# Attention's end: the second output weight unit split in one piece, recurrent high parts in every second step, three rows of h reloaded later

## What is computed

```
q, k, v, xr, gr = jnp.split(hl @ w_in, splits, axis=-1)
att = neighbourhood_attention(heads(q), heads(k), heads(v), kc, vc, rpb)
...
rec, rec_c = bidir_rglru(xr, xc, ...)
y = jnp.concatenate([att, rec * jax.nn.gelu(gr)], axis=-1) @ w_out
...
h = h + g1 * y
h = h + g2 * swiglu(modulate(rmsnorm(h, norm2_g[l]), sh2, sc2), ffn_w_gu[l], ffn_w_down[l])
```

## Time and profile before

| | |
|---|---|
| median of 3 runs | 2519.69 us (2513.82 to 2519.84) |
| profiled execution: its time, its span | 2521.1 us, 2519.0 us |
| PE busy, share of the span | 2442.0 us, 97% |
| DVE, ACT, POOL busy | 1125.8, 525.9, 1058.0 us |
| granted TensorE clock, mean | 0.986 of full speed |

### The profile page before, as it was taken

One profiled execution on the slowest core, in us unless ns is written; L12 is line 12 of the kernel. 1 busy time (PEld: TensorE's weight loads), 2 busy tenths in 40 slices (PEclk: granted clock), 3 DMA queues, 4 the chain that ended last, 5 costly groups with the idle time before them and its releaser, 6 DMA issues.

```text
span 2519.0 us, 29518 instructions
## 1 busy us (share of the span) xinstructions
PE 2442.0 (97%) x11190; PEld 1997.2 (79%) x11190; DVE 1125.8 (45%) x1447; ACT 525.9 (21%) x805; POOL 1058.0 (42%) x507
## 2 busy tenths in 40 slices
PE   7999999989899999999999999999899999999999
PEld 3778878878788888888887788887688888888887
DVE  6566648855744444422223534246622222222224
ACT  2444438861200000000002200002200000000003
POOL 3233336888533344444333233432533333333340
PEclk8999999999999999999999899999899999999999
DMA  9433366523323333211111011111211111111111
GB/s 290 156 130 131 136 174 137 102 96 106 108 95 115 117 117 106 94 42 49 42 50 51 26 42 50 50 50 34 59 47 46 49 43 50 42 49 50 50 34 67
DMA packets 223197, 206.54 MB, mean 82 GB/s; under 512 B 40119, under 2 KB 193427, under 8 KB 222611
## 3 DMA queue, kind: packets, MB, share of 16 engines
q1 hardware_dynamic: 216643, 186.64, 25.2%
q10 hardware_dynamic: 5904, 16.78, 1.8%
q0 software_dynamic: 576, 2.10, 0.2%
HBM read 185.20 MB, written 20.28 MB: 82 GB/s over the span
## 4 chain that ended last, share of the span: by engine, by line
PE 90%; DVE 5%; issue 2%; ACT 1%; DMA 1%; POOL 0%; SPq 0%; DVEq 0%; POOLq 0%; ACTq 0%
PE bank L757 28%; PE bank L759 27%; PE bank L758 27%; PE bank L889 1%; DVE probs L1659 1%; PE bank L945 1%; PE bank L818 1%; DVE sumsq L1378 1%; PE bank L971 1%; PE bank L970 1%; PE bank L932 1%; PE bank L789 1%; ACT probs L1262 1%; PE bank L933 1%; DVE h L1421 1%
## 5 line engine op out<-in xcount | busy, mean ns | idle before, releaser
L591 POOL TENSOR_TENSOR w_hi<-raw,ones 128x1024 fp32r<-128x1024 f32 x184 | 361.6, 1965 | 1221.3 <-PE bank L759 1166.0
L757 PE MATMUL bank<-act_hi,w_hi 128*128 128x512 f32 x2160 | 846.0, 392 | 3.5 <-DVE act_lo L1539 2.9
L758 PE MATMUL bank<-act_hi,w_lo 128*128 128x512 f32 x2168 | 847.5, 391 | 0.0
L759 PE MATMUL bank<-act_lo,w_hi 128*128 128x512 f32 x2160 | 843.0, 390 | 0.0
L757 PEld LDWEIGHTS bank<-act_hi,w_hi 128*128 128x128 f32 x2160 | 407.4, 189 | 91.0 <-issue 2.8
L758 PEld LDWEIGHTS bank<-act_hi,w_lo 128*128 128x128 f32 x2168 | 409.4, 189 | 84.3
L759 PEld LDWEIGHTS bank<-act_lo,w_hi 128*128 128x128 f32 x2160 | 407.1, 188 | 85.4
L594 POOL TENSOR_TENSOR w_lo<-raw,w_hi 128x1024 fp32r<-128x1024 f32 x184 | 468.1, 2544 | 14.5
L1421 DVE SCALAR_TENSOR_TENSOR h<-bank,mods,h 128x512 f32<-128x512 f32 x432 | 319.5, 748 | 218.5 <-PE bank L759 217.3
L1699 DVE TENSOR_TENSOR hid_f<-silu_g,bank 128x512 f32<-128x512 f32 x88 | 60.5, 687 | 710.6 <-PE bank L759 709.4
L757 PE MATMUL bank<-hid_hi,w_hi 128*128 128x512 f32 x704 | 277.1, 394 | 3.6 <-DVE h L1421 3.4
(11 more groups left out here) (212 smaller groups left out, 2397.3 us busy)
## 6 DMA issues: line engine op xcount, KB each, us to landing
raw<-in_ffn_w_gu SPq DMA_DIRECT2D x88, 512.0 KB, 3.8
mod_in_f<-in_mod_w SPq DMA_DIRECT2D x48, 512.0 KB, 4.7
raw<-in_ffn_w_down SPq DMA_DIRECT2D x44, 512.0 KB, 3.6
mod_in_p<-in_mod_w SPq DMA_DIRECT2D x32, 512.0 KB, 6.7
raw<-in_o_w_in SPq DMA_DIRECT2D x24, 512.0 KB, 3.7
raw<-in_e_w_in SPq DMA_DIRECT2D x20, 512.0 KB, 4.9
mod_ring<-in_mod_w SPq DMA_DIRECT2D x16, 512.0 KB, 9.5
raw<-in_e_w_out SPq DMA_DIRECT2D x16, 512.0 KB, 3.7
```

What stands on the lines that cost most here:

```text
L591: nc.gpsimd.tensor_tensor(w_hi, raw[:, parity, :], ones[:, 0:1].to_broadcast([P, UNIT]), ALU.mult).then_inc(s_hi, 1)
L757: pe.matmul(dst, w_hi, x_hi, start=first, stop=False)
L758: pe.matmul(dst, w_lo, x_hi, start=False, stop=False)
L759: return pe.matmul(dst, w_hi, x_lo, start=False, stop=last)
```

## The change

Four things are moved. The second output unit gets a low part of its own, `o_lo1`, which lies on the key buffer of the even heads and on rows 4 and 5 of `h`; so POOL splits unit 1 in one piece, ahead of block 13, once the scores and minima of the seventh head are done. Unit 5 waits for block 14 instead of PE's second output group. ACT writes the recurrent high parts behind the exponentials of steps 51, 53, 55 and 57 instead of 55 to 58, and POOL takes each low part one place earlier relative to its blocks. SP reloads rows 3 to 5 of `h` only when PE has done its second output group, between the loads of units 3 and 4.

```diff
-        o_lo0 = at(91, "o_lo0", [P, UNIT], F32R)
+        o_lo = [at(91, "o_lo0", [P, UNIT], F32R), at(18.5, "o_lo1", [P, UNIT], F32R)]
...
-            return (o_hi[0][:], o_lo0[:]) if j == 0 else (o_hi[1][:], w_lo4[:, 1, :]) if j == 1 else w_slot(j % 4)
+            return (o_hi[j][:], o_lo[j][:]) if j < 2 else w_slot(j % 4)
...
             sp.wait_ge(s_sc, STEPS)
             sp.dma_start(h[:, 0:3, :], h_spill[:, 0:3, :]).then_inc(s_reload[0], 16)
-            sp.dma_start(h[:, 3:6, :], h_spill[:, 3:6, :]).then_inc(s_reload[1], 16)
             sp.wait_ge(s_pt, STEPS)
             sp.dma_start(h[:, 6:8, :], h_spill[:, 6:8, :]).then_inc(s_reload[2], 16)
             for j in range(2, 2 * FT):
                 load_unit(U_O + j, j % 2, column_unit(w_out, (j % FT) * P))
+                if j == 3:
+                    sp.wait_ge(s_out, 2)
+                    sp.dma_start(h[:, 3:6, :], h_spill[:, 3:6, :]).then_inc(s_reload[1], 16)
...
-                if j < 6:
-                    pool.wait_ge(*((s_pv, 3 * BLOCKS // 4), (s_min, STEPS - TT), (s_pv, BLOCKS - 1), (s_yf, BLOCKS),
-                                   (s_pv, BLOCKS - 1), used_o(1))[j])
+                if j == 0:
+                    pool.wait_ge(s_pv, 3 * BLOCKS // 4)
+                elif j == 1:
+                    pool.wait_ge(s_min, STEPS - TT)
+                    pool.wait_ge(s_sc, STEPS - TT)
+                elif j < 6:
+                    pool.wait_ge(*((s_yf, BLOCKS) if j == 3 else (s_pv, BLOCKS - 1)))
...
-                if STEPS - 10 <= j < STEPS - 6:
-                    lru_high(j - STEPS + 10)
+                if STEPS - 14 <= j < STEPS - 6 and j % 2 == 0:
+                    lru_high((j - STEPS + 14) // 2)
```

More of the change, by code:

```diff
@@ L692, in out_weight @@
                 pool.wait_ge(s_hi, U_O + j + 1)
[L693 to L699, removed]
                 nc.gpsimd.tensor_tensor(w_lo, raw[:, j % 2, :], w_hi, ALU.subtract).then_inc(s_split, 1)
@@ L716, in _ @@
                     split_values(head // 2)
+                if head == HEADS - 1:
+                    lru_low(0)
                 y_low(2 * head - 3)
             out_weight(0)
-            lru_low(0)
+            lru_low(1)
             y_scaled(BLOCKS - 4)
-            lru_low(1)
+            lru_low(2)
             y_low(BLOCKS - 4)
-            lru_low(2)
+            out_weight(1)
             y_scaled(BLOCKS - 3)
@@ L726, in _ @@
             y_low(BLOCKS - 3)
[L727 to L732, removed]
+            for g in (BLOCKS - 2, BLOCKS - 1):
+                y_scaled(g)
+                y_low(g)
             for j in range(2, 2 * FT):
```

## The result

The changed kernel takes 2530.80 us (median of 6 runs, 2528.99 to 2534.43) where the kernel before takes 2519.77 (6 runs beside it). The ratio is 1.0043, 95% interval 1.0033 to 1.0054: 8.3 to 13.6 us slower. 2528.9 had been forecast. The profiled execution, at 2528.99 us, is the fastest of the six; no trace was kept of the others.

What follows compares the result with a forecast made beforehand. PE (TensorE), with 90% of the span in the chain, was taken as the bound. Terms 10.8 - 2.8 + 0 + 1.2 = +9.2 us on the profiled 2521.1, 1.4 above the median, gave 2528.9 us; range 2523.5 to 2533.0.

Steps and rivals of the forecast that it cites:

- Step 1: At ACT's first recurrent high part, moved ahead of its wait for POOL's last key/query split: ACT stands 8.99 us, paid whole.
- Step 2: At ACT's cast of block 11's y: extra copy +1.03, recovery -1.5, clock +2.3; shift with stall +10.8, bounds +7.5 to +13.0.
- -1.5 recovered, +2.3 for the clock: Up to block 11: ACT's waits for DVE go in part, -1.5 us; PE's low clock behind the stall costs +2.3.
- Step 3: POOL's chain from block 11 to unit 0's second half on PE: 33.6 us where it was 36.4, so -2.8.
- Step 4: PE's clock behind the 2.0 us wait ahead of unit 0's second half: 0 taken, upper bound +2.4 us.
- the rival "+11.6": The clock falls at attention's end too: sum +11.6 us, 2531.3; no chance of its own given.
- Step 5: SP's queue: unit 4's load behind the late reload of h makes PE wait +1.2 us, bounds 0 and +2.
- everything behind moves along: The norm and the loops behind attention shift with PE's groups; no further term was added for them.
- The rival without a stall: ACT reaches the copy after POOL's split; unit 0 gains up to 4.0, total -2.8 us, 2516.9; little or no stall 0.06.

Runs made afterwards that it cites:

- b: The kernel before with only ACT's four recurrent high parts moved to steps 51, 53, 55 and 57; ratio 1.0029 to the kernel before.
- h: The kernel before with the four recurrent high parts at steps 53, 55, 57 and 59; ratio 1.0026 to the kernel before.
- f: g with the four recurrent high parts spread to steps 55, 57, 59 and 61; ratio 0.9993 to the kernel before.
- g: The changed kernel with the edits of a and c together, leaving unit 1 split in one piece; ratio 0.9998 to the kernel before.
- w: The changed kernel with 36 zero-weight products added on PE during the stall; ratio 1.0058 to the kernel before.
- a: The changed kernel with ACT's four recurrent high parts back at steps 55 to 58; ratio 1.0010 to the kernel before.
- c: The changed kernel with unit 4's load issued ahead of the late reload of h's three rows; ratio 1.0029 to the kernel before.
- x: f with the last block's scaling and low part on DVE instead of POOL; ratio 0.9988 to the kernel before.
- y: x with POOL waiting for the last low part of y before it splits unit 2; ratio 0.9981 to the kernel before.

## Why the prediction was right, step by step

**Step 1, ACT's stall.** Forecast 8.99 us, 8.83 measured; b has it alone, and h shows that its price goes with its length.

**Step 2, what else moves the restart.** Forecast +10.8 at block 11, +9.87 measured. The wait and the extra copy make 8.83 + 1.03 = 9.86; f against g has 0.94 for a copy less. So the pair "-1.5 recovered, +2.3 for the clock" was mis-sized: together they are 0.0. By w the clock is 0.8 of it, which leaves -0.8 for what was recovered. The clock had been given 2.3, by PE's busy share of the whole stage, but behind the stall ACT had nearly as much to do as PE at its low clock.

**Step 3, POOL's tail.** Forecast -2.8; 61.33 - 54.08 = +7.25 at the second half, less 9.87, is -2.6, and a has -2.65 without the stall. The two waits it named, for the fourth recurrent low part (1.2 forecast, 1.1) and for the last low part of y (2.0, 2.1), are there.

**Step 4, the clock behind the shorter wait.** Forecast 0, with 2.4 as the upper bound. It was 0 in the changed kernel's profile, but the 12 products took 1.2 to 1.6 us more in a, c, g, f and x, behind a wait of 2.1 to 2.4. So that the term came out as 0 is luck: one place in the program has it both ways, and the rival "+11.6" is open for the five executions of which no trace was kept.

**Step 5, the late reload.** Forecast +1.2, measured 1.7. PE's second output group ended (T) at about 568.3, and POOL could begin unit 4 8.2 us later, not 8.0. The fourth update didn't wait, as forecast.

**The sum.** 9.87 - 2.62 + 0 + 1.71 = +9.0 up to unit 4, where 9.2 was forecast. What failed is the sentence that everything behind moves along: PE's wait in the norm grew from 7.69 to 8.97, 1.3 us more. The prediction had counted DVE's low parts as PE's followers and had not asked what POOL would be doing beside them. With it the terms make 10.2, and the norm's mark shows 10.14. The mechanism was right, then, but the closeness of the number is in part luck: the shift at block 11 was forecast 0.9 too high, and unit 4, the tail and the norm together 2.0 too low. Between the medians lie 11.0 us, 1.8 more than forecast.

The rival without a stall was priced too well: it gave unit 0's second half 4.0 us, and left out the wait for the fourth recurrent low part that step 3 itself had named. g, which has no stall, is 2.6 us ahead there.

## What to carry to other kernels

Before moving a step earlier on an engine that takes its work in order, read when its own wait is released: here the time by which it came too early was paid in full, and about 1 us with it. When a removed wait gives back less than its size, look for the chain that is late next; here that chain could be shortened (y), and the wait for it fell from 2.1 to 0.7 us. A transfer that is put ahead of a load in one queue can cost a second time far behind, when an engine that falls behind loses the pauses in which its neighbour ran fast.

## What was not expected of the hardware

- DVE's low part of 128x512 took 2.88 us when it began inside a POOL instruction and 0.74 when it began in a pause of POOL; that of 64x512 took 2.08 and 0.69. The slow ones ended 0.54 to 0.56 us behind that POOL instruction.
- The clock fell behind the same 2.1 us of idling in some kernels and not in others: 12 products took 4.4 us in a, c and g and 4.1 in f, but 2.9 in the changed kernel and in w.
- The start of the program is not equally long in each execution: up to step 51 it took 498.86 to 504.15 us in kernels that do not differ there. PE's wait for `x_diag`, 8.3 us before and 4.6 in the changed kernel, is the largest part of it that its waits show.
